# Rotary products between value tiles, the overflow experts' weights in two transfers, and the second block's sines inside the last expert loop

## What is computed

```python
# first model, per layer i
h = rmsnorm(x, g_mix[i]);  u = h @ w_in[i]
sb_q, sb_k, sb_v, da_q, da_k, da_v, gate_a, gate_b = split(u)
y_a = stick_breaking_attention(sb_q, sb_k, sb_v) @ w_br_a[i]
dq, dk = apply_partial_rope(da_q, cos, sin), apply_partial_rope(da_k, cos, sin)
y_b = rmsnorm(differential_attention(dq, dk, da_v, lam)) @ w_br_b[i]
x = x + (sigmoid(gate_a) * y_a + sigmoid(gate_b) * y_b) @ w_o[i]
x = x + hierarchical_moe(rmsnorm(x, g_ffn[i]), ...)     # 32 experts, 2 a token
x = x + (p[i] @ w_ple[i]) * sigmoid(rmsnorm(x, g_ple[i]) @ w_ple_gate[i])
# second model, the mixer
cq, ckv, kr, dq, dk, dv, g = split(u @ w_in)
q = rope(rms_norm(cq) @ w_uq)      # 8 heads of 96, the last 32 rotated
k = [rms_norm(ckv) @ w_uk, rope(kr)];  v = rms_norm(ckv) @ w_uv
o_a = dense_attention(q, k, v)
o_b = dilated_mixture(rope(dq), rope(dk), dv)
```

## Time and profile before

| | |
|---|---|
| median of 3 runs | 3460.74 us (3460.09, 3460.74, 3470.79) |
| profiled execution, whole / span | 3464.25 / 3462.5 us |
| PE / PE weight load busy | 91% / 52% |
| DVE / ACT / POOL busy | 35% / 16% / 17% |
| chain that ended last | PE 83%, DVE 8%, DMA 5%, issue 2%, ACT 2%, POOL 1% |
| mean granted clock of PE | 0.955 of full |

### The profile page before, as it was taken

How to read it: one execution, slowest core, us unless ns; L and a number is a source line. 1 busy time by engine, 2 the same in 40 slices (tenths; PEclk the granted TensorE clock), 3 DMA queues, 4 the chain that set the end, 5 groups by cost and what they waited for, 6 DMA issues and landing times.

```text
span 3462.5 us, 29709 instructions
## 1 busy us (share of the span) xinstructions
PE 3160.0 (91%) x11784; PEld 1812.6 (52%) x11784; DVE 1198.0 (35%) x2044; ACT 569.5 (16%) x918; POOL 591.6 (17%) x475
## 2 busy tenths in 40 slices
PE   7999998999699999898999699999898999899997
PEld 3656434333235555343333268888353434388886
DVE  2145433111331244423111554451333355344442
ACT  1022221111110032301111130000202233210010
POOL 0000010222000000011221124443100000144443
PEclk9999998999899999898999899999899999999998
DMA  4211112798712111123998422222221110222220
GB/s 165 74 49 37 49 55 73 304 366 347 294 61 73 61 37 49 37 79 128 365 364 345 164 73 87 92 90 96 69 71 37 49 61 27 71 73 85 85 98 25
DMA packets 76298, 412.64 MB, mean 119 GB/s; under 512 B 21184, under 2 KB 21312, under 8 KB 29568
## 3 DMA queue, kind: packets, MB, share of 16 engines
q1 hardware_dynamic: 56144, 387.67, 30.0%
q0 software_dynamic: 20016, 23.06, 1.9%
HBM read 513.41 MB, written 31.46 MB: 157 GB/s over the span
## 4 chain that ended last, share of the span: by engine, by line
PE 83%; DVE 8%; DMA 5%; issue 2%; ACT 2%; POOL 1%; SPq 0%; DVEq 0%; POOLq 0%; ACTq 0%
PE PS L781 23%; PE PS L442 21%; PE PS L465 12%; PE PS L724 7%; PE PS L452 4%; DMA BIG<-in_experts,ATT 4%; PE PS L746 4%; PE PS L497 1%; PE PS L565 1%; PE PS L522 1%; PE PS L700 1%; PE PS L509 1%; PE PS L611 1%; PE PS L620 1%; DVE ATT L981 1%
## 5 line engine op out<-in xcount | busy, mean ns | idle before, releaser
L442 PE MATMUL PS<-HT,ring 128*128 128x512 f32 (+1 forms) x1024 | 445.2, 596 | 10.5 <-DVE HT L1039 5.9
L465 PE MATMUL PS<-HT,ring 128*128 128x512 f32 x768 | 343.5, 600 | 0.2
L442 PEld LDWEIGHTS PS<-HT,ring 128*128 128x128 f32 (+1 forms) x1024 | 195.0, 191 | 260.1 <-issue 251.1
L465 PEld LDWEIGHTS PS<-HT,ring 128*128 128x128 f32 x768 | 143.6, 192 | 171.4 <-issue 165.8
L724 PE MATMUL PS<-ring,G 128*64 128x512 f32 x1024 | 231.1, 605 | 2.2 <-ACT G L2027 2.2
L781 PE MATMUL PS<-HT,ring 128*128 128x256 f32 x832 | 195.2, 387 | 21.0 <-ACT HT L1887 15.5
L781 PE MATMUL PS<-G,ring 128*128 128x256 f32 x880 | 208.2, 379 | 0.0
L2285 POOL TENSOR_TENSOR ATT<-ring 128x512 f32<-128x512 f32 (+1 forms) x68 | 85.0, 1250 | 656.4 <-PE PS L781 449.3
L781 PEld LDWEIGHTS PS<-HT,ring 128*128 128x128 f32 x832 | 161.0, 194 | 45.9 <-issue 12.7
L781 PEld LDWEIGHTS PS<-G,ring 128*128 128x128 f32 x880 | 167.2, 190 | 22.7
L781 PE MATMUL PS<-G,ATT 128*128 128x256 f32 x752 | 178.0, 379 | 0.0
(11 more groups left out here) (309 smaller groups left out, 4009.1 us busy)
## 6 DMA issues: line engine op xcount, KB each, us to landing
ring<-in_experts SPq DMA_DIRECT2D x192, 1024.0 KB, 9.0
ring<-in_stream SPq DMA_DIRECT2D x164, 1024.0 KB, 4.8
G<-expert_rows SPq DMA_DIRECT2D x8, 1024.0 KB, 7.9
h_tokens<-G POOLq DMA_DIRECT2D x2, 2048.0 KB, 8.2
XT<-in_xT SPq DMA_DIRECT2D x2, 1024.0 KB, 6.6
G<-in_pT POOLq DMA_DIRECT2D x2, 512.0 KB, 4.6
out_T<-XT SPq DMA_DIRECT2D x2, 512.0 KB, 3.6
G<-h_tokens,ATT POOLq DMA_INDIRECT x48, 8.1
```

What stands on the lines that cost most here:

```text
L442: mm = pe.matmul(ps[0:m, :], wv[:, k, c:c + m], rhs[:, k, :], start=k == 0, stop=k == nk - 1)
L465: mm = pe.matmul(ps, w[:, k, c:c + P], rhs[:, k, :], start=k == 0, stop=k == nk - 1)
```

## The change

Five things are altered.

- **Rotations between tiles.** `project_tokens` and the DVE helpers take a function that runs after each token tile. PE issues one rotation behind each of the eight value tiles (in the mixer two behind the first), and DVE's `rope` for it stands behind the store of that tile. The wait for the stored keys stands ahead of each rotation.
- **Heads.** The rotations of heads 0 to 3 stand behind the query products of heads 4 to 7, those of heads 4 to 7 behind the four key tiles.
- **Overflow weights.** The experts' weights lie in two arrays, gate and up in one, down in another. The tail's gate and up are loaded as soon as PE has finished gate and up of the tail step before; down is loaded where the whole was. Each has its own semaphore. The ring's loads of down read the second array.
- **Order in the expert loop.** PE turns the token rows of q+1 before gate and up of q, and ACT's copies run two steps ahead.
- **Sines.** The two tables are made inside the last layer's loop, on DVE after `rows` of steps 8 and 14, on ACT behind the gates of steps 9 and 15.

```diff
-            def project_tokens(w, nk, width, lhs):
+            def project_tokens(w, nk, width, lhs, between=lambda t: None):
...
-                unit_used("lin_ready")
+                    if t == TT - 1:
+                        unit_used("lin_ready")
+                    between(t)
...
+                    if q:
+                        pe.wait_ge(Q["x_copied"], at[f"moe{L}"]["x_copied"] + q)
                     pe.wait_ge(Q[g], now.next(g, 16))
...
                         if j == 0:
-                            pe.wait_ge(Q["tail_landed"], now.next("tail_landed", 32))
+                            pe.wait_ge(Q["tail_gu_landed"], now.next("tail_gu_landed", 32))
+                        if j == 2:
+                            pe.wait_ge(Q["tail_down_landed"], now.next("tail_down_landed", 32))
...
                 turn_x(0)
+                turn_x(1)
                 gate_up(0)
-                turn_x(1)
                 for q in range(1, NSEQ):
                     turn_hidden(q - 1)
-                    gate_up(q)
                     if q + 1 < NSEQ:
                         turn_x(q + 1)
+                    gate_up(q)
                     down(q - 1)
...
-                for n in range(2):
-                    project_tokens(unit(), KD, 256, HT)
-                pe.wait_ge(Q["lin_free"], qk)
-                rotate([DAQ[:, t, :] for t in range(4)] + [DAK[:, t, :] for t in range(4)], ROT)
+                for src in (DAQ, DAK):
+                    def rotate_one(t):
+                        pe.wait_ge(Q["lin_free"], qk)
+                        rotate([src[:, t, :]], ROT)
+                    project_tokens(unit(), KD, 256, HT, rotate_one)
...
+                    if t == 0 and src is DQ:
+                        rotate([KR], ROTM, DQK)
...
+            for h in range(4, 8):
+                head_query(w, h)
+                if h == 7:
+                    unit_used("lin_ready")
+                rotate_head(h - 4)
...
+            for t in range(4):
+                ps = lin_open()
+                for k in range(2):
+                    mm = pe.matmul(ps, w[:, k, t * P:(t + 1) * P], CKV[:, k, :], start=k == 0, stop=k == 1)
+                mm.then_inc(Q["lin_ready"], now.inc("lin_ready"))
...
+                rotate_head(4 + t)
...
-                if L == LAYERS - 1:
-
-                    v.wait_ge(Q["pos2_landed"], now.next("pos2_landed", 32))
-                    trig(COS[:, :], SIN[:, :], 1)
-                    trig(COSM, SINM, 2)
+                    if L == LAYERS - 1 and q == TRIG_AT[0]:
+                        v.wait_ge(Q["pos2_landed"], now.next("pos2_landed", 32))
+                        trig(COS[:, :], SIN[:, :], 1)
+                    if L == LAYERS - 1 and q == TRIG_AT[1]:
+                        trig(COSM, SINM, 2)
...
                 x_copy(0)
+                x_copy(1)
                 for q in range(NSEQ):
                     gate(q)
-                    if q + 1 < NSEQ:
-                        x_copy(q + 1)
-                if L == LAYERS - 1:
-                    trig(COS[:, :], SIN[:, :])
-                    trig(COSM, SINM)
+                    if q + 2 < NSEQ:
+                        x_copy(q + 2)
+                    if L == LAYERS - 1 and q == TRIG_AT[0] + 1:
+                        trig(COS[:, :], SIN[:, :])
+                    if L == LAYERS - 1 and q == TRIG_AT[1] + 1:
+                        trig(COSM, SINM)
...
+                    if 1 <= q < NSEQ and ORDER[q - 1][0] == "tail" and ORDER[q - 1][1] + 1 < TAILS:
+                        pool.wait_ge(Q["gu_ready"], 2 * (L * NSEQ + q))
+                        tail_gate_up(L, ORDER[q - 1][1] + 1)
                     if q >= 2:
                         pool.wait_ge(Q["y_ready"], y0 + q - 1)
                         scatter(q - 2)
                         kind, n = ORDER[q - 2]
                         if kind == "tail" and n + 1 < TAILS:
-                            tail_load(L, n + 1)
+                            tail_down(L, n + 1)
```

More of the change, by code:

```diff
@@ L2362, in experts @@
                         for side in range(2):
-                            load(A["experts"][L, 2 * m + side, :, j, :])
+                            e = 2 * m + side
+                            load(A["experts_gu"][L, e, :, j, :] if j < 2 else A["experts_down"][L, e, :, :])
             for L in range(LAYERS):
```

90 lines of the change are left out of this document (62 added, 28 removed).

## The result

The changed kernel takes 3388.1 us (median of 4 runs, 3384.55 to 3391.63), the kernel before 3465.8 us in the same comparison (3460.09 to 3485.36). The ratio is 0.9762, with a 95% interval of 0.9735 to 0.979: 2.4% faster. The forecast was 3394 us with a range of 3379 to 3410. The profiled execution took 3391.63 us with a span of 3389.8, which is 72.7 us under the span of before (3462.5). The forecast had 66.6 us, so it is 6 us short, and the experiments show that this small difference hides one large error. One execution of the kernel before, beside the last runs, took 5651.17 us at a granted clock of 0.553 and is in no median of this text.

A forecast was written before the change was run, and what follows sets the result against it. PE was taken as the bound, so its standstill and lower-clock time counted. Terms 9.6 + 9.6 + 5.1 + 9.7 + 7.2 + 25.2 - 0.7 + 0.9 = 66.6 us, off 3460.7, gave 3394 us, range 3379 to 3410.

The forecast's parts named there:

- Rotations in the layers: Value tiles to first logits, both layers: rotations between tiles hide DVE's work, 9.6 us less in each layer.
- The rival of no overlap: Value stages: each value tile waits 1.5 us for a rope, at most 28.9 us of gains go, 3423; chance 0.04.
- The clock behind them: Logits and gate tiles of layer 2: no fall to the lower clock after the rotations, 5.1 us less.
- Mixer: Mixer's value tiles to first scores: 11.6 us instead of 21.31, 9.7 less, with waits of 1.5 and 2.4.
- Heads: Last query to next scores in the mixer: DVE bounds the key tiles at 3.65 us each, 7.2 us less.
- The fall of the clock that the forecast feared here: Heads' key tiles: a clock fall makes them slower than DVE's copies, losing up to 3 us of the gain.
- Overflow weights: Tail steps of the expert loop: earlier split loads are hidden, all 14 PE waits go, 25.2 us less.
- The ring: Expert loop's weight loads: three steps need 33.6 us of transfers against 36.0 of steps, leaving 2.4 to spare.
- the rival of the ring: Expert loop: loads don't run closely, half of the 25.2 us returns as waits for down, 3407; chance 0.13.
- Order in the loop: Expert loop: no effect in steady state, 0.35 us worse at the start in each layer, -0.7 us.
- Sines: Last layer's loop: 2.86 us gained behind it, 2.0 lost to waits of 1.3 and 0.7, net 0.9 us.
- The 10.6 us: Sines in the last loop: cost of four table switches if Sin and Silu lay in different sets; sum 56, not 66.6.

The follow-up runs named there:

- e_weights: The kernel before with only the overflow weights split into two transfers, old loop order kept; 3435.0 us, ratio 0.9906.
- a_weights: The changed kernel with the overflow weights back in one transfer behind the scatter; 3387.3 us, ratio 0.976.
- a_short: The changed kernel with two of eight width slices left out of gate and up, same ring transfers; loop of layer 1 took 276.2 us.
- a_sines: The changed kernel with the sines back behind the last expert loop; one execution, loop of layer 2 took 292.9 us.
- e_order: The kernel before with only the new expert loop order, overflow weights still in one transfer; 3432.2 us, ratio 0.989.
- e_heads: The kernel before with only the head rotations moved between queries and key tiles; 3457.8 us, ratio 0.996.

## Why the prediction was right or wrong, step by step

- **Rotations in the layers: right.** 9.6 us each was forecast, 9.5 measured; tile and rotation at 4.31 us, no wait at any tile. The rival of no overlap falls.
- **The clock behind them: the mechanism right, the size a draw.** In layer 2 the 5.1 us came back. The same stretch became another 4.7 us shorter further on, where it spent 36 us at the lower clock instead of 46, and the one of layer 1 got 4.0 longer, with 47 us at the lower clock instead of 38. The profiles of the four kernels with the run of rotations, against the ten profiles without, show that the fall belongs to the run, and that the profile of before had caught one layer of two.
- **Mixer: right.** 9.7 forecast, 9.4 measured, waits of 1.36 and 2.33 us for 1.5 and 2.4. A short fall of the clock is still there behind the first scores.
- **Heads: mechanism right, 0.9 us too high.** The three rotations ahead of the last query cost 3.0 us instead of 2.7, and the key tiles come at 3.75 us and not 3.65. DVE was the bound as forecast, and its gaps between the steps of a rope and the two copies are a little larger than I had counted. The fall of the clock that the forecast feared here didn't come.
- **Overflow weights: the gain right, its cause half right.** All 14 waits went, and e_weights alone gives 27.2 us in the loops for the 25.2 forecast. But a_weights shows that the split wasn't needed once the order was changed. The step that failed was to treat it as a term of its own.
- **The ring: the floor right within 0.5 us.** 33.6 us was forecast for three steps' loads, a_short shows 34.1. That its slack of 2.4 us would last was wrong, because the steps became shorter: 4.4 us of waits came, as the rival of the ring describes, but a third of its size.
- **Order in the loop: this step failed.** The forecast was -0.7 us: "In the steady state turning the next token rows only changes its place". Alone it gives 33.4 us in the loops, 13.2 of them from 0.3 us in each of 22 steps of two layers, the rest because it makes all but one of the waits for the overflow weights go (24.1 us less, with 3.4 us more of waits for the ring). In the whole change, where these had gone anyway, taking it back costs 4.8 us in the loops against the first profile and 7.3 against the second. The start of the loop was told rightly, with a wait of 1.00 us for the hidden rows (1.05 forecast). The error was to count transposes by their columns alone and not to look at the weight loads, which showed the 0.81 us gap at both places in the kernel before. What was put at nothing is a cost of 0.3 us for each visit to the transposes.
- **Sines: the terms about right, the net not shown.** Down waits 1.2 and 1.2 us (1.3 and 0.7 forecast), and 17.9 us pass from the last result rows to the first addition where 20.9 did, so the net by these terms is 0.6 us for 0.9. But only 1.1 us arrived between the loop's end and the mixer's values, and a_sines, with the sines back behind the loop, takes 922.0 us for the two stretches together, between the 923.1 and 921.6 of the changed kernel's two profiles. The trace has no table load between the Silus and the sines, as before. The 10.6 us that the rule of the Trainium skill (ScalarE: Activation LUTs, What ACT_TABLE_LOAD costs) would have added for four switches of the set don't appear: that rule speaks of a switch, and there was none.

Why was the sum only 6 us off? The loops gave 30.5 us together where 25.2 - 0.7 - 2.0 = 22.5 was forecast for them, 8 us more. The heads, and the stretch behind the last loop (1.1 us gained of the 2.9 forecast there), gave 2.7 of it back. The stretches whose program the change leaves alone gave 6.4 us together where 5.1 were forecast, out of parts of +9.8, -4.0, -0.6, +1.4 and -0.2. The failed term was large by itself, but it overlapped with another one that was counted in full; that the two nearly make up for each other is luck, and so is the clock's part, which in another execution of the same kernel was 4 us different in one stretch alone. As for the times, the forecast started from 3460.7 us, the median of three executions; over all its runs the kernel before had a median of about 3470, and the medians gained 77 us and more. Part of what is beyond the 66.6 is probably the clock at the rotations, which the changed kernel no longer pays, but one profile of each kernel can't show it. The runs of the changed kernel also lie closer together (3384.2 to 3391.6) than those of before (3459.4 to 3485.4).

## What to carry to other kernels

When two edits shorten the same wait, cost each with the other in place: their gains don't add. When small transposes or products stand between large ones, look at the weight-load row for a gap at the first of them, and put such pieces together, so that the way in and back is paid once. Before you shorten PE in a loop that streams weights, work out the transfers' floor for the same number of steps: here 1.0 us in 35.1 was left, and the next savings in the loop mostly came back as waits for the ring.

## What the runs showed of the hardware

**About 0.15 us at each change between the whole array and its halves.** The loop's products have weights 64 columns wide, in pairs on the two halves of the array, and their loads stand 0.43 us apart. The load for 128 columns behind them stands 0.95 us behind. It isn't the transpose: in the changed kernel the value products of the mixer's attention (L615, 64 wide) are followed by ordinary products 96 wide (L942) with the same gap, and transposes behind products that are 128 wide (L469, then L569) have none. Nor is it the wide load: the narrow loads of L615 behind wide products (L469) have the gap too. The weight loads, in this order:

```profile
2712.38 0.14 PEld L615 LDWEIGHTS PS<-ATT,BIG 128*64 128x64 f32 x2 [0.28 <-issue]
2713.34 0.24 PEld L942 LDWEIGHTS PS<-BIG,ring 128*96 128x96 f32 x2 [0.81 <-issue]
```

```profile
2547.05 0.19 PEld L469 LDWEIGHTS PS<-HT,ring 128*128 128x128 f32 x1 [0.24 <-issue]
2547.48 0.14 PEld L569 LDWEIGHTS PS<-MATS,ATT 128*128 128x128 f32 x1 [0.24 <-issue]
```

```profile
2586.61 0.19 PEld L469 LDWEIGHTS PS<-HT,ring 128*128 128x128 f32 x1 [0.24 <-issue]
2587.55 0.20 PEld L615 LDWEIGHTS PS<-ATT,BIG 128*64 128x64 f32 x4 [0.76 <-issue]
```

The starts of PE's single records in the expert loop give the price. From one pair of products to the next pass 0.43 us, from one transpose to the next 0.11. At the way in it is 0.52 from the last pair to the first transpose and 0.17 to the second, together 0.15 too much. At the way back it is 0.21 from the last transpose to the first pair and 0.48 to the second, again 0.15 too much. The two make the 0.30 us of a visit. The same 0.52 us stands ahead of the logits, whose weights take half of the array's rows: from the last rotation's row at 198.75 us to theirs at 199.70 there are 0.95 us, where from such a row to the next value tile there are 0.85.

The Trainium skill (TensorE: Matmul & The Clock Gate, The mechanism) says that a load is pulled ahead of products in flight if it targets a row group that doesn't conflict, or the background weight buffer. The rows of 128 columns behind 128 agree with the second half of that: their load starts 0.43 us ahead of their product. At a change the load and its product start together (807.87 us for both at L742), in both directions, an exception that the sentence doesn't have. That the load isn't pulled ahead across a change is a reading of these rows; why is not shown.

**The cost of a fall of the clock is a draw.** The fall itself came in every profile with the run of rotations, but the logits and the four rows behind them paid 0 to 6 us. In layer 1 the kernels before, e_order, e_weights and e_heads have the same program up to there and reach the value tiles within 0.2 us of each other, and yet two of them paid and two didn't.
